# Sliding attention: the odd head's probabilities of each pair are scaled on GpSimd, the even head's on VectorE

## What is computed

```python
def attend(args):
    qb, kbb, vbb, mb = args
    sc = jnp.einsum('bqhgd,bkhd->bhgqk', qb, kbb).astype(F32) * scale
    sc = jnp.where(mb, sc, NEG_INF)
    m = jnp.maximum(jnp.max(sc, axis=-1, keepdims=True), sink)
    p = jnp.exp(sc - m)
    p = p / (jnp.sum(p, axis=-1, keepdims=True) + jnp.exp(sink - m))
    return jnp.einsum('bhgqk,bkhd->bqhgd', p.astype(vbb.dtype), vbb)
```

## Time and profile before

| | |
|---|---|
| time, median of 3 runs | 1389.41 us (1389.12 to 1390.63) |
| the profiled execution's own time | 1387.35 us |
| its span, first to last instruction | 1385.5 us |
| mean granted clock of TensorE, as a share of full speed | 0.995 |
| busy, share of the span: PE, PEld, DVE, ACT, POOL | 96%, 73%, 61%, 25%, 9% |
| the attention units: from 546 to 584 us of the span | |

### The profile page before, as it was taken

The page is one execution under the profiler, slowest core; times in us unless marked ns, Lnnn a source line. Parts: engine busy times, 40 slices in busy tenths (PEclk is TensorE's granted clock), DMA queues, the critical chain, the costliest instruction groups (busy, mean ns, idle before and its releaser), DMA issues. The chain is left out here.

```text
span 1385.5 us, 24951 instructions
## 1 busy us (share of the span) xinstructions
PE 1330.5 (96%) x10780; PEld 1012.3 (73%) x10780; DVE 849.8 (61%) x1424; ACT 353.2 (25%) x754; POOL 120.3 (9%) x184
## 2 busy tenths in 40 slices
PE   7999999899999998899999999998999999999999
PEld 6868548479996444559998467846788765999943
DVE  4678511147787356628988668458445364798973
ACT  3221201202221023513333013703433331233300
POOL 5745000000000011000000000031000000000000
PEclk9999999999999999999999999999999999999999
DMA  8343134054455525044445543400000042444442
GB/s 325 147 157 145 64 122 152 31 197 148 166 183 183 194 109 182 1 152 158 155 175 183 182 182 122 183 1 3 4 33 34 10 176 76 167 173 148 168 182 91
DMA packets 16733, 182.30 MB, mean 132 GB/s; under 512 B 1648, under 2 KB 3952, under 8 KB 6000
## 3 DMA queue, kind: packets, MB, share of 16 engines
q1 hardware_dynamic: 14320, 175.12, 34.7%
q10 hardware_dynamic: 2304, 5.59, 1.1%
HBM read 179.65 MB, written 1.05 MB: 130 GB/s over the span
## 5 line engine op out<-in xcount | busy, mean ns | idle before, releaser
L1619 PE MATMUL banks<-xn,arena 128*128 128x128 f32 x1440 | 165.7, 275 | 0.0
L1619 PEld LDWEIGHTS banks<-xn,arena 128*128 128x128 f32 x1440 | 163.2, 192 | 0.0
L1382 PE MATMUL banks<-weight_ring,arena 128*128 128x512 f32 x288 | 126.3, 595 | 1.8 <-ACT arena L1012 1.0
L1636 PE MATMUL banks<-arena 128*128 128x512 f32 x264 | 122.0, 592 | 0.0
L1619 PE MATMUL banks<-hT,weight_ring 128*128 128x128 f32 x960 | 116.5, 275 | 0.0
L1619 PEld LDWEIGHTS banks<-hT,weight_ring 128*128 128x128 f32 x960 | 111.8, 192 | 0.0
L1382 PEld LDWEIGHTS banks<-weight_ring,arena 128*128 128x128 f32 x288 | 54.6, 192 | 67.5 <-issue 65.9
L1636 PEld LDWEIGHTS banks<-arena 128*128 128x128 f32 x264 | 49.8, 190 | 60.7 <-issue 60.7
L1636 PE MATMUL banks<-weight_ring,arena 128*128 128x512 f32 x198 | 93.3, 592 | 0.0
L2523 DVE SCALAR_TENSOR_TENSOR arena<-arena,prm 128x255 f32<-128x255 f32 x200 | 87.3, 479 | 5.4 <-ACT arena L1029 3.6
L1029 ACT ACTIVATE arena<-arena,prm 128x256 f32<-128x256 f32 x100 | 54.6, 593 | 86.3 <-issue 44.2
(11 more groups left out here) (431 smaller groups left out, 2148.8 us busy)
## 6 DMA issues: line engine op xcount, KB each, us to landing
weight_ring<-in_wall SPq DMA_DIRECT2D x81, 2048.0 KB, 8.0
weight_ring<-in_wall SPq DMA_DIRECT2D x2, 1024.0 KB, 7.4
x<-in_x_tok ACTq DMA_DIRECT2D x2, 512.0 KB, 4.5
arena<-in_mem_tok SPq DMA_DIRECT2D x1, 1024.0 KB, 18.1
arena<-in_wall SPq DMA_DIRECT2D x1, 1024.0 KB, 5.0
arena<-in_wide SPq DMA_DIRECT2D x2, 512.0 KB, 4.8
out_y<-x ACTq DMA_DIRECT2D x4, 256.0 KB, 2.0
arena<-in_masks ACTq DMA_DIRECT2D x1, 896.0 KB, 9.4
```

What stands on the lines that cost most here:

```text
L1382: ins = mm(b_(n, width), lhsT=xT[:, kb, tt * P:(tt + 1) * P], rhs=wc[:, kb * 512 + c0:][:, :width], start=kb == 0, stop=kb == KB - 1)
L1619: ins = mm(b_(n)[:, j * P:(j + 1) * P], lhsT=weights[:, kb, j * P:(j + 1) * P], rhs=features_[:, kb, :], start=opens and j == 0 and kb == ...
L1636: ins = mm(b_(n), lhsT=a, rhs=b, start=pair == 0, stop=pair == FB // 2 - 1)
```

## The change

The reciprocal of a unit now raises a semaphore of its own, `sw_den`. VectorE waits for it (as it waited for its own step before) and scales only the two blocks of the even head. GpSimd waits for the same semaphore and scales the two blocks of the odd head in place, then raises `sw_p_odd`. TensorE's columns of a unit wait for both. On GpSimd unit 0's two multiplications stand between the inverse roots of the first and of the second token tile, and those of units 1 to 7 behind both.

```diff
@@ semaphores @@
         sw_p = sem("sw_p")
+        sw_den = sem("sw_den")
+        sw_p_odd = sem("sw_p_odd")
@@ TensorE, window_columns(u) @@
                 pe.wait_ge(sw_p, u + 1)
+                pe.wait_ge(sw_p_odd, u + 1)
                 free(n)
@@ VectorE, window_p(u) @@
                 do(tt_(den[:, at], den[:, at], dsk[:, at], ALU.add))
-                do(V.reciprocal(den[:, at], den[:, at]))
-                for m in range(4):
+                V.reciprocal(den[:, at], den[:, at]).then_inc(sw_den, 1)
+                dve.wait_ge(sw_den, u + 1)
+                for m in range(2):
                     part = w_p[:, (u % 4) * 1024 + m * T:][:, :T]
                     ins = ts_(part, part, den[:, 4 * u + m:4 * u + m + 1], None, ALU.mult)
                 ins.then_inc(sw_p, 1)
@@ GpSimd @@
                 inverse_root(qrs[:, 20 * tt + 12:][:, :8], qss[:, 20 * tt + 12:][:, :8], 8, HD, EPS, head_root)
+                for u in ((0,) if tt == 0 else range(1, 8)):
+                    pool.wait_ge(sw_den, u + 1)
+                    for m in (2, 3):
+                        part = w_p[:, (u % 4) * 1024 + m * T:][:, :T]
+                        ins = g.tensor_scalar(part, part, den[:, 4 * u + m:4 * u + m + 1], None, ALU.mult)
+                    ins.then_inc(sw_p_odd, 1)
```

## The result

The changed kernel takes 1394.68 us (median of 6, 1392.45 to 1396.08), the kernel before 1389.41 us (median of 6, 1387.29 to 1390.63): a ratio of 1.0037, 95% interval 1.0024 to 1.0050. It is **slower**, by 5.3 us or 0.37%. Forecast were 1390.0 us and no change; the range ended at 1393.0. Three executions of the experiments' kernels, two of e_reorder and one of e_warm_after, took 1976 to 2977 us; they lie far outside all others and are in none of the ratios.

What follows compares the result with a forecast made beforehand. The prediction took a latency loop through TensorE, not VectorE's busy time, as the bound. Four latencies of 0.14 us gave +0.6 us on 1389.41, so 1390.0 us and no change, range 1387.5 to 1393.0.

Steps and rivals of the forecast that it cites:

- The loop through TensorE: Attention units 4 to 6: columns, values, scores, mask, maximum and scaling form a latency loop of 8.01 us for two units.
- VectorE's 88%: VectorE's busy share in the attention units; the rival that it bounds claimed -3.7 us, chance 4 in 100.
- the four places: The scaled probabilities of units 1, 2, 4 and 6, where any change of latency counts four times.
- D: Length of one GpSimd scaling of 128x256, taken as 0.51 us, range 0.40 to 0.73.
- The rival with the dear instruction: GpSimd's scaling takes 0.79 us or more, adding 2.8 us, or 3.7 at 0.90; chance 7 in 100.
- The Trainium skill's price: GpSimd's scaling at best about 1.8 cycles an element: 0.67 us an instruction, +1.9 us in all.
- Taking turns: In the scaling, VectorE and GpSimd alternate on SBUF, one whole instruction each; unit 6's last block ends 0.14 us later.
- the formula: Added latency of a unit's scaling: d = 2 D - 0.88, giving +0.14 us.
- The second fall: TensorE's clock falls again behind the longer waits: +2.4 us in all, up to +4.1; chance 7 in 100.
- The sum: Four latencies of 0.14 us at units 1, 2, 4 and 6: +0.6 us, ends -0.3 and +2.3.
- the marks: Profile signs forecast: VectorE's mean over 0.35 us, GpSimd's 0.5 to 0.7, reciprocal to columns 1.4, waits 9.7, period 8.15.
- the three signs of being wrong: Two-unit period below 7.9 us, GpSimd's instruction over 0.8 us, or the clock's low stretch changing its length.

Runs made afterwards that it cites:

- e_reorder: Kernel before, with TensorE's values of two units moved behind the scores of the next step; ratio 0.9983 to the kernel before.
- e_warm_after: Changed kernel with 32, 20 and 28 idle transposes in TensorE's waits of units 1, 4 and 6; ratio 1.0015 to the kernel before.
- e_none: Changed kernel without GpSimd's scalings, the odd head left unscaled; ratio 0.9992 to the kernel before.
- e_product: Changed kernel with GpSimd's scaling written as a product with the broadcast column; ratio 1.0017 to the kernel before.
- e_slack: Changed kernel with GpSimd scaling the odd head only in units 0, 3, 5 and 7; ratio 1.0003 to the kernel before.
- e_alone: Changed kernel without VectorE's two scalings, the even head left unscaled; ratio 1.0050 to the kernel before.
- e_reorder_after: Changed kernel with TensorE's values moved behind the scores of the next step; ratio 1.0015 to the kernel before.
- e_constant: Changed kernel with GpSimd multiplying its two blocks by the constant 0.5; ratio 1.0047 to the kernel before.
- The two filled kernels: Kernel before and changed kernel, each with idle transposes in TensorE's waits of units 1, 4 and 6; ratios 0.9996 and 1.0015 to the kernel before.

## Why the prediction was wrong

**What bounds: right.** The loop through TensorE, not VectorE's 88%, and the four places through which the chain runs (at unit 1 in full only with the low clock behind it, as e_warm_after shows). e_none gave 2.01 us for 4 x 0.53, e_product 1.08, e_slack 0.15 with the other four units moved, and e_reorder the period of VectorE's own work once the values were out of the loop. In the changed kernel VectorE waits 3.39 us ahead of the mask of unit 7 (0.46 before):

```profile
578.63 0.70 DVE L2737 TENSOR_TENSOR banks<-banks,arena 128x512 f32<-128x512 f32 x1 [3.39 <-PE banks L1738]
```

**GpSimd's price: wrong, and this is the step that failed.** I took 0.51 us for D and 0.73 as its upper end, on the ground that an instruction with one stream can't cost more than one with two full streams. It measures 0.91 alone (e_alone) and 1.00 beside VectorE, and four times the missed latency, 4 x (0.93 - 0.14) = 3.2 us, is the larger part of what the sum lacks. The ground was the mistake: a row of another operation on the same engine bounded nothing. One column took 0.29, 256 take 0.91, so 2.4 ns a column, where the copy whose rate I used has 0.84; the whole product takes 0.62 to 0.73 us. The rival with the dear instruction was priced rightly, 4 x (2 D - 0.88), which is +3.8 us at D = 0.91; 4 x 0.93 = 3.7 us was measured. Its chance of 7 in 100 was far too low, since no row spoke for the price at all.

**The Trainium skill's price**, from which the prediction drew an estimate of 0.67 us, is too low as well for this form. The 1.8 cycles stand in the GPSIMD Engine Reference as the best case of a loop, in section 3.1, "Elementwise — side-by-side cycle accounting", and not in 2.1, which the prediction names; 0.91 us is measured.

**Taking turns: right in size, wrong in kind.** The rule that each instruction holds the way to SBUF for its whole length would have VectorE's second scaling end behind GpSimd's first, which ended at 582.45. It ended at 582.14. With the product in its place VectorE does wait it out (below). By the formula d is 0.94 at D = 0.91, and 0.93 is measured, but that is in part luck. What happens is simpler: GpSimd starts 0.09 us behind the reciprocal, its two instructions follow each other in 1.98 us, 0.16 more than alone, and TensorE starts 0.10 us behind them, where I took 0.06.

**The clock: named, and too small.** The second fall had 7 in 100 and came not once but twice. The columns and values of unit 4 took 4.33 us to the next work instead of 2.95, those of unit 6 4.28 instead of 2.95: 1.38 and 1.33 us. I had argued from the one wait of 2.90 us behind which it did not fall. At unit 6 the length of the wait doesn't decide: the clock fell behind 2.27, 2.33 and 2.38 us (e_slack, e_reorder_after, e_none) and not behind 2.34 and 2.90 us (e_reorder, before). So that the fall at unit 6 is the change's doing isn't shown. At unit 4 the unfilled kernels are of one mind: it fell behind 2.62, 2.64 and 2.78 us (e_constant, e_alone, changed) and in no kernel with a wait of 2.12 us or less there. So in this stage a longer wait can carry a price of its own, which belongs into the forecast and not into a corner of it; what decides it stays open.

**The sum.** 3.72 us of latency, 1.38 and 1.33 of low clock make 6.43 of the 6.59 us of the stage. The rest, 0.16, is mostly where the turned heads behind unit 1 run at low clock. The two filled kernels, with what the filling ran on and the 1.44 us of unit 2 taken off, differ by 46.3 - 43.1 = 3.2 us; by them latency and clock have about half each, since part of the latency at unit 1 counts only through the low clock. The medians differ by 5.3, with 3.3 to 6.9 in the interval. The granted clocks of the 82 executions show that the kernel before has further falls in some of them, and its profiled execution is 2.06 us under its median; so the profiled pair shows somewhat more than the medians. Which falls those executions had, no trace shows.

**Which of the marks were met.** VectorE's mean is 0.46 (over 0.35, as forecast), but GpSimd's is 1.00 and not 0.5 to 0.7. The reciprocal-to-columns distance is 2.17 and not 1.4. The waits are GpSimd's, at three of the four places, and take 12.4 us together and not 9.7. The period of two units is 10.33 us from unit 4 to unit 6 and not 8.15. Of the three signs of being wrong, two came: GpSimd's instruction takes over 0.8 us, and the low clock changed its length.

## What to carry to other kernels

Ask of an engine that is 88% busy whether it ever waits in the loop; if it does, count the latency of what is moved, not its busy time, and only at the places through which the chain runs. Price an operation on another engine by a row of that very operation at that width; without one, the upper end is open and the chance of it large. Where TensorE waits for microseconds, a longer wait can cost a second time through the clock of the matmuls behind it, and a few idle transposes in the wait can buy some of it back, if they end before it does: 2.29 us of the changed kernel's stage here, while the kernel before gained nothing clear of the scatter.

## What was not expected of the hardware

GpSimd multiplies 128x256 f32 by a constant (0.92 us beside VectorE) or by a scalar from a column (1.00 beside VectorE, 0.91 alone) more slowly than by a second tensor, which here is the same column broadcast (0.64 beside VectorE).

The two forms also treat VectorE differently. Beside the products, VectorE's first scaling of unit 6 took 0.80 us and both took 1.42, while GpSimd's two took 1.23, which is twice the 0.617 of the earlier trace rows: GpSimd wasn't hindered. Rows of e_product, VectorE's first, VectorE's two, GpSimd's two:

```profile
576.07 0.80 DVE L2751 TENSOR_SCALAR arena<-arena,small 128x256 f32<-128x256 f32 x1
576.07 1.42 DVE L2751 TENSOR_SCALAR arena<-arena,small 128x256 f32<-128x256 f32 x2
...
576.11 1.23 POOL L3143 TENSOR_TENSOR arena<-arena,small 128x256 f32<-128x256 f32 x2 [3.05 <-DVE small L2747]
```

Beside the slower tensor-by-scalar form VectorE's two took 0.83, and 0.62 with GpSimd idle (e_none). The Trainium skill's rule (SBUF — State Buffer, section "SBUF: two separate sides"; the page ties it to certain forms of VectorE's instruction, and of which form this scaling is no row here tells), that the shared pair is held for the whole instruction and the loser fully blocks, fits the lengths of the first case, though not who wins: the page gives the pair to whoever starts first, and VectorE's scaling, issued 0.04 us ahead of GpSimd's product, was the one that waited. In the second case the measurement decides, and VectorE's second scaling, 0.35 us alone, ended 0.48 us behind its first and 0.31 us ahead of the end of GpSimd's instruction, which had begun before it. What GpSimd does in the time in which it leaves VectorE alone, no run here shows.
